# Gates of 192 tokens through a DRAM grid, in place of one-hot products for 128

## The reference

```
q = (x @ w_q).reshape(C, 8 heads, 2, 128)
s = einsum("chpd,hpnd->chpn", q, subkeys)            # 128 first keys, 128 second keys
top_s, top_i = top_k(s, 16)                          # for each half
best_s, best_pos = top_k(sums of the pairs, 16)      # 16 experts per token and head
ia, ib = first and second key of each; expert = ia * 128 + ib
g = softmax(best_s)
act = gelu(einsum("chkd,cd->chk", u[expert], x)) * g
y = einsum("chk,chkd->cd", act, v[expert])
```

## Time and profile before

| | us |
|---|---|
| median of 3 runs | 1883.57 |
| the profiled execution | 1886.6 |
| its span (first to last instruction) | 1884.8 |

### The profile page before, as it was taken

How to read it: one execution, slowest core, us unless ns; L and a number is a source line. 1 busy time by engine, 2 the same in 40 slices (tenths; PEclk the granted TensorE clock), 3 DMA queues, 4 the chain that set the end, 5 groups by cost and what they waited for, 6 DMA issues and landing times.

```text
span 1884.8 us, 37910 instructions
## 1 busy us (share of the span) xinstructions
PE 1866.2 (99%) x12642; PEld 1655.2 (88%) x12642; DVE 1492.7 (79%) x2893; ACT 1001.2 (53%) x1598; POOL 783.3 (42%) x378
## 2 busy tenths in 40 slices
PE   8999999999999999999999999999999999999999
PEld 7999998888888888887789999988888888888887
DVE  6758999999778977997765489988887678668866
ACT  4354555555555555554454645555555555555553
POOL 3877548788860000000062575487888820000000
PEclk8999999999999999999998999999999999999999
DMA  9986657898897777876632565577777776667664
GB/s 352 364 271 202 187 136 185 229 225 230 229 244 245 257 233 236 264 233 225 223 114 83 170 200 168 136 159 182 184 179 189 190 215 194 187 193 215 190 191 140
DMA packets 174340, 388.82 MB, mean 206 GB/s; under 512 B 48801, under 2 KB 84001, under 8 KB 173857
## 3 DMA queue, kind: packets, MB, share of 16 engines
q1 hardware_dynamic: 120960, 379.01, 64.0%
q0 software_dynamic: 36864, 0.15, 4.7%
q10 hardware_dynamic: 16416, 8.39, 1.6%
HBM read 377.92 MB, written 9.57 MB: 206 GB/s over the span
## 4 chain that ended last, share of the span: by engine, by line
PE 92%; DVE 4%; DMA 2%; ACT 1%; issue 1%; POOL 1%; DVEq 0%; SPq 0%; ACTq 0%; POOLq 0%
PE bank L673 36%; PE bank L658 18%; PE bank L663 9%; PE bank L637 6%; PE bank L642 6%; PE bank L638 6%; PE bank L692 2%; PE bank L704 1%; DMA raw<-in_v_panels 1%; PE bank L720 1%; PE bank L522 1%; PE bank L502 1%; PE bank L953 1%; PE bank L504 1%; PE bank L503 1%
## 5 line engine op out<-in xcount | busy, mean ns | idle before, releaser
L1012 ACT CAST w_hi<-raw 128x1024 fp32r<-128x1024 f32 (+1 forms) x603 | 630.5, 1046 | 327.9 <-PE bank L673 104.0
L1414 DVE TENSOR_TENSOR w_lo<-raw,w_hi 128x1024 fp32r<-128x1024 f32 x488 | 596.9, 1223 | 192.4 <-PE bank L673 88.5
L1389 POOL DMA_INDIRECT gates_by_expert<-g_t,place x256 | 504.9, 1972 | 190.0 <-DVE place L1713 76.4
L1361 POOL TENSOR_TENSOR w_lo<-raw,w_hi 128x1024 fp32r<-128x1024 f32 (+2 forms) x115 | 273.3, 2380 | 528.3 <-PE bank L673 381.4
L658 PE MATMUL bank<-act_two,w_hi 128*128 128x512 f32 x1536 | 379.3, 389 | 0.0
L658 PEld LDWEIGHTS bank<-act_two,w_hi 128*128 128x128 f32 x1536 | 288.3, 188 | 59.8
L673 PE MATMUL bank<-w_hi,wt_hi 128*128 128x512 f32 x1024 | 325.5, 398 | 1.9 <-DVE wt_lo L1676 1.2
L673 PE MATMUL bank<-w_lo,wt_hi 128*128 128x512 f32 x1024 | 317.9, 391 | 0.0
L673 PE MATMUL bank<-w_hi,wt_lo 128*128 128x512 f32 x1024 | 317.0, 390 | 0.0
L637 PE MATMUL bank<-act_two,w_hi 128*128 128x256 f32 x984 | 246.1, 288 | 0.0
L638 PE MATMUL bank<-act_two,w_hi 128*128 128x256 f32 x984 | 241.2, 283 | 0.0
(11 more groups left out here) (257 smaller groups left out, 1951.2 us busy)
## 6 DMA issues: line engine op xcount, KB each, us to landing
raw<-in_u_panels SPq DMA_DIRECT2D x256, 512.0 KB
raw<-in_v_panels SPq DMA_DIRECT2D x256, 512.0 KB
raw<-in_panels SPq DMA_DIRECT2D x81, 512.0 KB
ada<-in_ada_rows SPq DMA_DIRECT2D x56, 512.0 KB
arena<-in_ada_rows SPq DMA_DIRECT2D x40, 512.0 KB, 7.0
gates_by_expert<-zero ACTq DMA_DIRECT2D x2, 4096.0 KB, 22.2
arena<-gates_by_expert SPq DMA_DIRECT2D x32, 256.0 KB, 5.3
gates_by_expert<-g_t,place POOLq DMA_INDIRECT x256
```

Of the source, the lines that this page charges most:

```text
L1012: nc.scalar.copy(w_hi[:, slot, 0:width], raw[:, slot, 0:width]).then_inc(hi_done, 1)
L1361: pool.tensor_tensor(w_lo[:, lo_slot, 0:width], raw[:, slot, 0:width], w_hi[:, slot, 0:width].bitcast(F32), ALU.subtract).then_inc(lo_done, 1)
L1389: pool.indirect_dma_start(grid[l], bass.IndirectOffsetOnAxis(place[:, n:n + 1], 0), kept[:, n:n + 1], None, compute_op=ALU.add).then_inc(a ...
L1414: dve.tensor_tensor(w_lo[:, lo_slot, 0:width], raw[:, slot, 0:width], w_hi[:, slot, 0:width].bitcast(F32), ALU.subtract).then_inc(lo_done, 1)
```

## The change

- The grid now holds three sets of 64 tokens (`SETS`, `SET`): sets 0 and 1 are the first 128 tokens, in `grid0`; set 2 is the next 64, in `grid1`. Set 0 is used by quarters 1 to 3, set 1 by quarters 2 and 3, set 2 by quarter 3.
- `BY_GRID = (2, 4, 6)`: loops q = 0, 1, 2 have 2, 4 and 6 iterations without blocks by matmul. Loop 0 thus has 12 blocks instead of 16, loop 1 has 8 as before, loop 2 has 4 instead of 8.
- `turn_back` runs once per set: sets 0 and 1 before panel 12, set 2 before panel 15 (`BACK`). Each consists of 4 bf16 products and 2 fp32 ones (the gates are now turned back as well), 64 columns each. ScalarE does 3 instructions per set, VectorE one. The 64 tokens lie on two halves of the partitions (half of each head's ranks on each), so that one indirect DMA still carries 128 gates and a set takes 64 of them.
- The adds: 192 per layer instead of 128, and a wait after every 8 instead of every 16. GpSimd counts them per set.
- The clear: quarters 1 and 2 of `grid0` (4 MB) where the old one stood, then quarter 3 of `grid0` (2 MB) and of `grid1` (1 MB) at panel 12 of the search.
- The fetch: in every loop SyncE waits before iteration 6 (`FETCH_FROM`) for the set that the quarter needs last, then issues half of the quarter's DMAs before the loads of iteration 6 and half before those of iteration 7. Quarter 1 takes 8 DMAs of 64 tokens (256 B pieces), quarter 2 takes 8 of 128 tokens (512 B pieces), quarter 3 takes 8 of 128 tokens and 8 of 64. Before, it was 3, 3 and 2 DMAs of 128 tokens before iterations 5, 6 and 7 of loops 1 and 2. The grid is stored with the second key outermost, before with the first key outermost.

```diff
-BACK = 15
+BACK = {12: (0, 1), 15: (2,)}
-BLOCKS = 48
-NTH = {0: 16, 1: 24, 2: 32}
-BY_GRID = 4
+SET = 64
+SETS = 3
+BLOCKS = 40
+BY_GRID = (2, 4, 6)
+FETCH_FROM = (6, 6, 6)
+CLEAR_AT = 12
...
@@ SyncE
-                with sp.Fori(0, 8) as it:
-                    mix_loads(0, it)
-                for q in (1, 2):
-                    with sp.Fori(0, BY_GRID) as it:
+                for q in range(3):
+                    first = FETCH_FROM[q]
+                    with sp.Fori(0, first) as it:
                         mix_loads(q, it)
-                    mix_loads(q, BY_GRID)
-                    if q == 1:
-                        sp.wait_ge(added[HEADS - 1], 16 * TOPK * (l + 1))
-                    sp.wait_ge(w_mul, 64 * l + 16 * q)
-                    for g, parts in enumerate(((0, 1, 2), (3, 4, 5), (6, 7))):
-                        for n in parts:
+                    sp.wait_ge(added[q], 16 * SET * (l + 1))
+                    if q:
+                        sp.wait_ge(w_mul, 64 * l + 16 * q)
+                    for it in range(first, 8):
+                        for n in range((it - first) * 8 // (8 - first), (it - first + 1) * 8 // (8 - first)):
                             load_grid(q + 1, n)
-                        mix_loads(q, BY_GRID + 1 + g)
+                        mix_loads(q, it)
...
@@ load_grid
+                    by_key = lambda grid, w: grid.rearrange("(p a t) o -> p a (t o)", p=P, t=w)[:, a:a + 4]
+                    sp.dma_start(to[:, :, 0:tokens], by_key(grid0[l], P)[:, :, 0:tokens]).then_inc(s_grid, 16)
+                    if quarter == 3:
+                        sp.dma_start(to[:, :, P:P + SET], by_key(grid1[l], SET)).then_inc(s_grid, 16)
...
@@ TensorE
-                def turn_back():
-                    pe.wait_ge(idx_copied, TT * (l + 1))
+                def turn_back(g):
+                    pe.wait_ge(idx_copied, TT * l + g // 2 + 1)
+                    bank = BACK_BANK[g]
+                    halves = lambda a: a.rearrange("p (h e i) -> p e h i", h=HEADS, e=2)
                     for n, numbers in enumerate((ia_t, ib_t)):
-                        by_rank = numbers[:, 0:P * DUP].rearrange("p (t r) -> p t r", r=DUP)[:, :, 0]
-                        mm = pe.matmul(SC[0][:, n * P:(n + 1) * P], by_rank, ident_b[:], start=True, stop=True)
+                        by_rank = numbers[:, g * SET * DUP:(g + 1) * SET * DUP].rearrange("p (t r) -> p t r", r=DUP)[:, :, 0]
+                        for e in range(2):
+                            pe.matmul(bank[e * SET:(e + 1) * SET, n * SET:(n + 1) * SET], by_rank, halves(ident_b[:])[:, e],
+                                      start=True, stop=True)
+                    for e in range(2):
+                        mm = pe.matmul(bank[e * SET:(e + 1) * SET, 2 * SET:3 * SET], g32_t[:, g * SET:(g + 1) * SET],
+                                       halves(ident)[:, e], start=True, stop=True)
                     mm.then_inc(back_done, 1)
...
@@ ScalarE
+                    if i == CLEAR_AT:
+                        clear(grid0, 3 * QUART, KEYS)
+                        clear(grid1, 3 * QUART * SET // P, KEYS * SET // P)
...
@@ GpSimd
+                pool.wait_ge(s_zero, 48 * (l + 1))
+                for g in range(SETS):
+                    grid = (grid0, grid0, grid1)[g][l]
+                    pool.wait_ge(place_ready, SETS * l + g + 1)
+                    pool.wait_ge(gates_kept, SETS * l + g + 1)
+                    for h in range(HEADS):
+                        for n in range(g * SET + h * TOPK // 2, g * SET + (h + 1) * TOPK // 2):
+                            pool.indirect_dma_start(grid, ...place[:, n:n + 1]..., kept[:, n:n + 1], None,
+                                                    compute_op=ALU.add).then_inc(added[g], 16)
+                        pool.wait_ge(added[g], 16 * SET * l + 16 * TOPK // 2 * (h + 1))
```

More of the change, by code:

```diff
@@ L117, in program @@
     ctx = ExitStack()
-    grid = [nc.dram_tensor(f"gates_by_expert{l}", (KEYS * KEYS * P, 1), F32, kind="Internal").ap() for l in range(2)]
+    grid0 = [nc.dram_tensor(f"gates_of_tile0_{l}", (KEYS * KEYS * P, 1), F32, kind="Internal").ap() for l in range(2)]
+    grid1 = [nc.dram_tensor(f"gates_of_tile1_{l}", (KEYS * KEYS * SET, 1), F32, kind="Internal").ap() for l in range(2)]
     with ctx:
@@ L278, in program @@
         s_zero = sem("gate_grid_zeroed")
-        added = [sem(f"gates_of_head{h}_added") for h in range(HEADS)]
+        added = [sem(f"gates_of_set{g}_added") for g in range(SETS)]
         s_grid = sem("gates_from_grid_landed")
@@ L773, in mix_body @@
                             v_panel(f"mix{l}", j + 3, 8, it, s, 1)
[L775 to L778, removed]
+                for q in range(3):
+                    with pe.Fori(0, BY_GRID[q]) as it:
                         mix_body(q, it, False)
-                    with pe.Fori(BY_GRID, 8) as it:
+                    with pe.Fori(BY_GRID[q], 8) as it:
                         mix_body(q, it, True)
@@ L1119, in turned, with row_starts @@
                     i.then_inc(gates_spread, 1)
[L1121 removed]
+                def row_starts(g):
                     act.wait_ge(tokens_ready, 1)
[L1124 to L1127, removed]
+                    act.wait_ge(back_done, SETS * l + g + 1)
+                    bank, c = BACK_BANK[g], slice(g * SET, (g + 1) * SET)
+                    for e in range(2):
+                        p = slice(e * SET, (e + 1) * SET)
+                        col = 1 - e + g % 2
+                        i = nc.scalar.activation(row_start[p, c], bank[p, SET:2 * SET], ACT.Identity,
+                                                 bias=tok[p, col:col + 1], scale=float(KEYS * (P if g < 2 else SET)))
+                    if g == 2:
+                        act.wait_ge(gate_parts, TT * (l + 1))
+                    nc.scalar.copy(kept[:, c], bank[:, 2 * SET:3 * SET]).then_inc(gates_kept, 1)
                 for j in range(AHEAD - EARLY):
@@ L1175, in peer @@
                 for q in range(3):
[L1176 to L1179, removed]
+                    with act.Fori(0, BY_GRID[q]) as it:
+                        mix_body(q, it, False, False)
+                    with act.Fori(BY_GRID[q], 7) as it:
                         mix_body(q, it, False, True)
@@ L1699, in experts, with places @@
             def experts(l):
+                def places(g):
+                    dve.wait_ge(gates_kept, SETS * l + g + 1)
+                    bank, c = BACK_BANK[g], slice(g * SET, (g + 1) * SET)
+                    dve.scalar_tensor_tensor(out=place[:, c], in0=bank[:, 0:SET], scalar=float(P if g < 2 else SET),
+                                             in1=row_start[:, c], op0=ALU.mult, op1=ALU.add).then_inc(place_ready, 1)
+                for g in BACK[12]:
+                    places(g)
                 for j in range(SCATTER, AHEAD - EARLY):
@@ L1710, in experts @@
                         gate_part(l, 1)
-                    if j == BACK:
-                        dve.wait_ge(start_ready, l + 1)
-                        dve.scalar_tensor_tensor(out=place[:], in0=SC[0][:, 0:P], scalar=float(KEYS * P), in1=row_start,
-                                                 op0=ALU.mult, op1=ALU.add).then_inc(place_ready, 1)
+                    for g in BACK.get(j, ()):
+                        places(g)
                 weigh(0, 0, BLOCKS * l + 16 + 2)
```

65 lines of the change are left out of this document (30 added, 35 removed).

## The result

| | before | after |
|---|---|---|
| median, 5 runs each on one chip (us) | 1885.61 | 1893.43 |
| ratio, 95% interval | | 1.0044 (1.0028 to 1.0061) |
| profiled execution (us) | 1886.6 | 1891.69 |
| its span (us) | 1884.8 | 1889.9 |

The change makes the kernel slower by 0.44%, about 8 us. A later series gave 1892.47 against 1884.58 us, 1.0045 (1.0029 to 1.0061). The prediction said 1878.2 us and a range of 1875 to 1885: it was wrong.

A forecast was written before the change was run, and what follows sets the result against it. TensorE, busy 99% of the span, was taken as the bound. Blocks -9.1, turning back +2.9 and fetch +0.8 gave -5.4 us, so 1883.6 became 1878.2 us, range 1875.0 to 1885.0.

The forecast's parts named there:

- Blocks by matmul: Loops 0 and 2, both layers: 16 blocks removed at 0.57 us each take 9.1 us off TensorE's path.
- Rival 4: Loops 0 and 2: the blocks were not on the path, so removing them gives nothing; 1887 us, chance 0.03.
- Turning back: TensorE in "ahead": the added bf16 and fp32 products per set cost 2.9 us in both layers (1.9 to 4.2).
- Waits in ahead: ScalarE's and VectorE's new small instructions delay the one-hots some 0.6 us, covered by 1.6 us; cost nothing, 1.2 at most.
- The clears: Panel 12 of the search: ScalarE's wait of 1.56 us covers two issues; cost 0, bounds 0 to 0.5 us per layer.
- SyncE's wait for the adds: Before iteration 6 of loop 0: set 0 is complete 14 us before SyncE's wait in layer 1; cost 0.
- rival 2: Loop 0: adds late for set 0, SyncE waits and TensorE stalls 19 us in layer 1; 1897 us, chance 0.03.
- The fetch: Loop 2 bursts of 5.6 to 7.5 us against layer 0's 3.9 us margin: 0.8 us in all, 5.2 at most.
- rival 1: Loop 2: late panels use up the gain, costing 5.2 us at 38 ns per packet; 1882.6 us, chance 0.21.
- ScalarE's wait of 6 to 8 us for the panel: Sign in loop 2: ScalarE waits 6 to 8 us instead of 3.2 for a panel of U behind the fetches.
- TensorE's idle time of at most 1 us: Sign in loop 2: TensorE is idle at most 1 us where ScalarE waits for a panel of U behind the fetches.
- Rival 3: Fetches of loops 2 and 0: 256 B pieces cost twice a 512 B packet, 18 us of stalls; 1895 us, chance 0.09.

The follow-up runs named there:

- the repeat: The changed kernel run once more, unchanged, beside the kernel before: 1892.47 us (nine runs) against 1884.58, ratio 1.0045.

## Why the prediction was wrong, step by step

- **Blocks by matmul, -9.1 us.** Right: -8.9 us in the four places. Rival 4 (not on the path) falls.
- **Turning back, +2.9 us.** Right in kind, a little dear: 2.5 us (0.86 and 0.48 in layer 0, 0.65 and 0.47 in layer 1).
- **Waits in ahead, 0.** Right for the start: six ScalarE instructions came before the one-hots (at 249.67), and the block of TensorE at 253.86 shows no wait.
- **The clears, 0 (bound 0.5 per layer).** Wrong, 3.7 to 3.9 us in the two layers. The step took an issue for a constant of 0.3 to 0.5 us, from rows in which the queue was nearly empty. The third clear was issued behind 4096 pieces and took 7.00 us. The experiment that moved it shows this. The 1.56 us in which ScalarE waited for TensorE could cover two issues of 0.37 us and not one of 7.
- **SyncE's wait for the adds, 0.** Right. The adds of set 0 in layer 1 ended at 1358.92 + 1.54 us, SyncE's first grid load came at 1373.88, 13 us later; rival 2 falls. Both came 9 us later than forecast, for the losses of layer 0 and of the search stand ahead of both. The last add of set 2 started at 1716.34, some 18 us before it was needed.
- **The fetch, +0.8 us (to 5.2).** This is the step that failed. It was a comparison of a burst with a margin. The burst was sized by packet times, 5.6 to 7.5 us against 2.8 for the old one. In the packet records the two new bursts of layer 0 took 7.3 and 8.6 us, the old one of the earlier trace rows 5.2, and the panel of U was cast 2.7 and 5.0 us later than in the earlier trace rows, where 2.8 to 4.7 was forecast. So the size of the burst was nearly right, and the margin was wrong: 3.9 us holds for the cast of the panel of U alone. TensorE stopped for the low part of the V panel behind it, 2.17 us in the first burst although the panel of U came within that margin, and 2.46 us in the second. The 8 issues at 0.5 us were named and left out; the fifth took 2.60 and 3.88 us, which goes with gaps in the transfers of the second burst only. Last, the clock fell, which no term held (1.7 us). Together it is 7.8 us in place of 0.8, and 6.4 to 9.8 in five other profiles of the same bursts. That is rival 1 (late panels in loop 2), with its place right and its price, 5.2 us, too small by a third; and 1.4 us of that price had been put on layer 1, which lost nothing. Of the signs that the prediction named, ScalarE's wait of 6 to 8 us for the panel came true (6.45 us), and TensorE's idle time of at most 1 us did not (2.17 us).
- **A sign that was overlooked.** The trace of before shows issues that are no constant: at 766.46 us a panel of U behind three grid loads took 1.37 us to issue, where a panel otherwise takes 0.33, and at 608.42 the third load of a burst took 1.21 us. The earlier trace rows happened to show a panel that took 0.35.
- **Rival 3 (pieces of 256 B dear)** falls. There are 32 loads of such pieces in the changed kernel (16 per layer), not 24 as the prediction says. Their 16384 pieces of 256 B took 18.6 ns each in the packet records, those of 512 B 28 to 30 ns. The narrow pieces did not make the burst slower than the wide ones. The Trainium skill, "DMA: Bandwidth & Descriptors", Specifications, asks for 512 B for line rate: per byte the trace agrees, 74 ns per KB against some 58; an extra cost on top of that, as if each piece were read and written back, is not seen.
- **The end of ahead** was not a step at all: 2.0 us in the first profile, tied to how TensorE's waits stand there, cause open.

In numbers: -8.9 + 2.5 + 3.7 + 2.0 + 7.8 = +7.1 us, where -5.4 was forecast. The clears and the end of ahead account for 5.7 us of the difference, the fetch for 7.0. The chance of 0.14 for slower had been put on rivals 2 to 4; none of them happened.

## What to carry to other kernels

Price an issue by what already stands in its queue: a transfer of many small pieces is cheap to issue only while few are outstanding, and behind them the issuing engine stops with everything it still has to do. Put such transfers one by one between the loads that they share the queue with, and never on a compute engine behind a big one of its own. A margin read for one late panel does not cover the panel behind it: follow the engines' program order from the late cast to the next product, and take the smallest slack on that way.

## What the runs showed of the hardware

- The engine that issues a DMA is held while many pieces are outstanding in its queue: 7.00 us on ScalarE behind 4096 pieces; 2.60 to 3.88 us on SyncE at the fifth transfer of 512 pieces in layer 0, 2.66 us with pieces half as wide, at most 1.20 us with half as many. It is let go before they are all moved (2782 of 4096 on ScalarE, 720 of 2048 on SyncE in the first burst).
- An idle time of 2.2 us on TensorE, after hundreds of us at 2.4 GHz, was followed by some 3.4 us at 1.2 GHz (mean granted clock 0.77 and 0.69 in the windows above), which added 1.7 us to the stall. It is not so after each: 2.46 us idle in the same trace was followed by none, and in the repeat both bursts were.
- TensorE's signal at the end of a group of products can come 0.8 to 1.1 us later than the products' pace says, with one arrangement of the waits behind it (13 of 16 layers) and not with others (0 of 12). The same two waits in the kernel before did not bring it. Why is open.
